# Two heads per stationary matrix in the levels of a blockwise triangular inverse (two hybrid layer stacks, one core)

## What is computed

```python
kk = jnp.einsum("bhnid,bhnjd->bhnij", k_beta, kc)
lower = jnp.eye(c, dtype=f32) + jnp.where(strict, kk * decay, 0.0)
rhs = jnp.concatenate([vc * bc[..., None], k_beta * jnp.exp(G)[..., None]], axis=-1)
uw = lax.linalg.triangular_solve(lower, rhs, left_side=True, lower=True)
```

## Time and profile before

| | |
|---|---|
| median of 3 runs | 2100.92 us (2100.28 to 2102.86) |
| the profiled execution | 2102.94 us, its span 2101.1 us |
| PE busy | 1967.9 us (94% of the span) |
| DVE busy | 802.2 us (38%) |
| ACT busy | 448.8 us (21%) |
| POOL busy | 433.2 us (21%) |
| granted TensorE clock, mean of the span | 0.958 of 2.4 GHz |
| share of the chain that ended last: PE | 87% |
| levels of the first layer of the second stack | 1554.78 to 1616.51 us |
| levels of the second layer | 1950.13 to 2011.86 us |

### The profile page before, as it was taken

The page is one execution under the profiler, slowest core; times in us unless marked ns, Lnnn a source line. Parts: engine busy times, 40 slices in busy tenths (PEclk is TensorE's granted clock), DMA queues, the critical chain, the costliest instruction groups (busy, mean ns, idle before and its releaser), DMA issues.

```text
span 2101.1 us, 25762 instructions
## 1 busy us (share of the span) xinstructions
PE 1967.9 (94%) x10102; PEld 1192.8 (57%) x10102; DVE 802.2 (38%) x1957; ACT 448.8 (21%) x1213; POOL 433.2 (21%) x463
## 2 busy tenths in 40 slices
PE   7999997999996999897989996999999989999997
PEld 4566555555553566555545553546679544556973
DVE  2735345122113734436212123235554323455534
ACT  4333211111112333210111111122310112232011
POOL 0101302433431101311324331001330000024000
PEclk9999897999997999997989998999899999999999
DMA  5121067999933121065999965120020021101100
GB/s 214 35 83 41 0 272 276 422 395 366 375 141 148 54 83 41 1 270 183 415 400 387 393 257 212 40 80 31 31 81 1 32 90 73 48 31 71 41 1 40
DMA packets 52824, 323.39 MB, mean 154 GB/s; under 512 B 20876, under 2 KB 22188, under 8 KB 29920
## 3 DMA queue, kind: packets, MB, share of 16 engines
q1 hardware_dynamic: 33344, 292.28, 35.2%
q0 software_dynamic: 19360, 29.45, 3.9%
HBM read 404.21 MB, written 30.93 MB: 207 GB/s over the span
## 4 chain that ended last, share of the span: by engine, by line
PE 87%; DVE 5%; DMA 4%; ACT 1%; issue 1%; POOL 0%; SPq 0%; POOLq 0%; DVEq 0%; ACTq 0%
PE bank L932 14%; PE bank L562 14%; PE bank L2188 11%; PE bank L2174 8%; PE bank L950 8%; PE bank L574 4%; PE bank L2159 4%; DMA b_nat<-xn_rows,b_rows_ix 3%; PE bank L2349 3%; PE bank L2340 3%; PE bank L548 2%; PE bank L2280 2%; PE bank L914 2%; PE bank L2277 2%; PE bank L2151 1%
## 5 line engine op out<-in xcount | busy, mean ns | idle before, releaser
L932 PE MATMUL bank<-b_arena,b_nat 128*64 128x256 f32 x3008 | 345.8, 383 | 3.7 <-DVE b_nat L1412 3.7
L562 PE MATMUL bank<-b_arena 128*128 128x512 f32 (+2 forms) x768 | 308.6, 556 | 2.6 <-issue 2.2
L932 PEld LDWEIGHTS bank<-b_arena,b_nat 128*64 128x64 f32 x3008 | 219.2, 139 | 154.1 <-issue 61.0
L1412 DVE TENSOR_TENSOR b_nat<-bank,b_prm 128x512 f32<-128x512 f32 x94 | 65.1, 693 | 438.3 <-PE bank L914 330.3
L2188 PE MATMUL bank<-b_actT,b_ring 128*128 128x512 f32 x512 | 224.0, 594 | 0.0
L562 PEld LDWEIGHTS bank<-b_arena 128*128 128x128 f32 x768 | 145.3, 194 | 137.2 <-issue 107.4
L950 PE MATMUL bank<-b_arena,b_ebuf 128*64 128x512 f32 x752 | 185.4, 614 | 1.9 <-ACT b_ebuf L1253 1.9
L2174 PE MATMUL bank<-b_ring,b_actT 128*128 128x384 f32 (+1 forms) x512 | 177.1, 504 | 7.6 <-DVE b_actT L3028 7.6
L2188 PEld LDWEIGHTS bank<-b_actT,b_ring 128*128 128x128 f32 x512 | 96.0, 190 | 114.9 <-issue 113.8
L1385 POOL DMA_INDIRECT y_rows<-b_va,b_rows_ix x94 | 95.8, 1019 | 313.4 <-ACT b_va L1261 305.7
L2174 PEld LDWEIGHTS bank<-b_ring,b_actT 128*128 128x128 f32 x512 | 98.8, 196 | 78.6 <-issue 33.0
(11 more groups left out here) (363 smaller groups left out, 2577.8 us busy)
## 6 DMA issues: line engine op xcount, KB each, us to landing
b_arena<-in_w SPq DMA_DIRECT2D x64, 2048.0 KB, 15.0
b_arena<-in_w SPq DMA_DIRECT2D x64, 1024.0 KB, 17.1
b_ring<-in_w_t SPq DMA_DIRECT2D x8, 2048.0 KB
b_arena<-in_w SPq DMA_DIRECT2D x8, 1536.0 KB, 15.8
b_ring<-in_w_n2b SPq DMA_DIRECT2D x6, 1536.0 KB
b_arena<-in_w_out SPq DMA_DIRECT2D x4, 2048.0 KB
b_arena<-y_rows SPq DMA_DIRECT2D x8, 1024.0 KB, 7.9
b_ring<-in_w_out SPq DMA_DIRECT2D x4, 2048.0 KB
```

The lines of the kernel that those rows point to most:

```text
L562: ins = pe.matmul(bank[:, 0:width], actT[:, k, tok(i)], w[:, k, :], start=k == 0, stop=k == KD - 1)
L932: ins = pe.matmul(psum[2 + b % 2][f * CAP:(f + 1) * CAP, 0:256], xgT[:, b % 2, k % 4, k // 4, :], w[:, k, f, :], start=k == 0, stop=k == K ...
```

## The change

The heads 0 and 1 are paired with the heads 2 and 3. L of one head lies below the diagonal, the transpose of L of the other above it, so the sum of both fits one 128 x 128 matrix. `first_inverse` builds it (`pairs[t]`, two matrices per chunk). For each level GpSimd multiplies it by a mask that now holds the level's blocks on both sides of the diagonal and writes `own[t]` (`level_part`). With it as the stationary matrix, one matmul of 128 columns gives the first product of one head (natural order, its 64 even-block columns) and of the paired head (transposed, its 64 odd-block columns): `mixed` describes these interleaved columns. The mask sits in the stationary matrix, so the product needs no masking, and ScalarE copies it out. A second ScalarE operation (`mix`) gathers the counterpart columns of the inverses into the other half of `t1`, which then serves as stationary and as moving operand. `inv` and `turned` (the transposes) of a chunk now lie side by side in `both[t]`. The copies of bank "lt" on ScalarE go.

The second matmul of the pair works on whole 128-column products: 4 matmuls of 128 columns in place of 8 of 64 (in the last level 4 of 64, as before). The order of PE, of the banks and of the chunks is kept.

```diff
@@ constants
         if n == 0:
             c[:, CN["lvlt"]:CN["lvlt"] + P] = m.T
+        else:
+            c[:, CN["lvl"] + n * P:CN["lvl"] + (n + 1) * P] = m | m.T
@@ block_two
-        lt = [by_heads(y[:, t, 0:DW]) for t in range(T)]
+        pairs = [y[:, t, 0:2 * P].rearrange("p (h s) -> p h s", h=2) for t in range(T)]
...
+        both = [ring[2][:, 2 * t * DW:2 * (t + 1) * DW].rearrange("p (s j) -> p s j", j=P) for t in range(T)]
+        inv = [both[t][:, 0:DH, :] for t in range(T)]
+        turned = [both[t][:, DH:2 * DH, :] for t in range(T)]
+        squares = [ring[2][:, n * DW:(n + 1) * DW] for n in range(4, 8)]
...
+        own = [y[:, t, 2 * P:4 * P].rearrange("p (h s) -> p h s", h=2) for t in range(T)]
...
+        def mixed(heads, n, pair=None):
+            b = 1 << n
+            ap = heads if pair is None else heads[:, pair, :]
+            blocks = (P if pair is None else P // 2) // b
+            return bass.AP(ap.tensor, ap.offset, [list(heads.ap[0]), [2 * b, blocks], [2 * P + b, 2], [1, b]])
@@ level_one (PE)
-                four(l, "t1", lambda h: lt[t][:, h, :], lambda h: inv[t][:, tok(h)], T * (n - 1) + t)
+                s = T * (n - 1) + t
+                pe.wait_ge(*after(l, "own", s + 1))
+                pe.wait_ge(*vacant(l, "t1", s))
+                bank, full = writer(l, "t1", s)
+                for c in range(2):
+                    ins = pe.matmul(bank[:, tok(c)], own[t][:, c, :], mixed(inv[t], n, c), start=True, stop=True)
+                ins.then_inc(*full)
@@ level_two (PE)
                 pe.wait_ge(*emptied(l, "t1", s))
-                if n > 1:
+                if n < LEVELS - 1:
+                    pe.wait_ge(*after(l, "mixed", s + 1))
...
                 if n < LEVELS - 1:
-                    for h in range(DH):
-                        pe.matmul(bank[:, 64 * h:64 * (h + 1)], by_heads(invT[t])[:, h, :],
-                                  level_cols(t1[s % 2][:, h, :], n, 0), start=True, stop=True)
-                for h in range(DH):
-                    ins = pe.matmul(bank[:, 256 + 64 * h:256 + 64 * (h + 1)], t1[s % 2][:, h, :],
-                                    level_cols(invT[t][:, tok(h)], n, 1), start=True, stop=True)
+                    for c in range(2):
+                        pe.matmul(bank[:, tok(c)], t1[s % 2][:, 2 + c, :], t1[s % 2][:, c, :], start=True, stop=True)
+                    for c in range(2):
+                        ins = pe.matmul(bank[:, tok(2 + c)], t1[s % 2][:, c, :], t1[s % 2][:, 2 + c, :],
+                                        start=True, stop=True)
...
@@ run_scalar
-                copy_out(l, "lt", lt[0], 0)
-                copy_out(l, "lt", lt[1], 1)
...
-                for t in range(T):
-                    copy_out(l, "yg", actT[:, DH:KD, tok(t)], t, scale=prm[:, l, PC2["glag"]:PC2["glag"] + 1])
+                def mix(s):
+                    n, t = 1 + s // T, s % T
+                    if n > 1:
+                        act.wait_ge(*after(l, "invT", s - T + 1))
+                    else:
+                        act.wait_ge(*after(l, "inv0", t + 1))
+                    if s >= 2:
+                        act.wait_ge(*filled(l, "up", s - 2))
+                    act.activation(t1[s % 2][:, 2:4, :].rearrange("p c (k w b) -> p (c k) w b", w=2, b=1 << n),
+                                   mixed(turned[t], n), ACT.Copy).then_inc(*did("mixed"))
+                for s in range(T * (LEVELS - 1)):
+                    if s < T * (LEVELS - 2):
+                        mix(s)
+                    copy_out(l, "t1", t1[s % 2][:, 0:2, :], s)
+                    if s % T == T - 1 and s < T * T:
+                        copy_out(l, "yg", actT[:, DH:KD, tok(s // T)], s // T,
+                                 scale=prm[:, l, PC2["glag"]:PC2["glag"] + 1])
@@ run_gpsimd
+            def level_part(l, s):
+                n, t = 1 + s // T, s % T
+                if n > 1:
+                    pool.wait_ge(*filled(l, "t1", s - T))
+                else:
+                    pool.wait_ge(*after(l, "inv0", t + 1))
+                pool.tensor_tensor(own[t], pairs[t], every(lvl[:, n, :], 2), ALU.mult).then_inc(*did("own"))
...
-                for t in range(T):
-                    gate_gla(l, t)
+                for s in range(T * (LEVELS - 1)):
+                    level_part(l, s)
+                    if s % T == T - 1 and s < T * T:
+                        gate_gla(l, s // T)
@@ first_inverse (DVE)
-                link(tt(by_heads(inv[t]), dn[t % 2], every(lvl[:, 0, :]), ALU.mult))
-                link(tt(by_heads(inv[t]), every(ident), by_heads(inv[t]), ALU.subtract))
-                dve.wait_ge(*emptied(l, "lt", t))
-                link(tt(by_heads(invT[t]), lt[t], every(lvl[:, LEVELS, :]), ALU.mult))
-                tt(by_heads(invT[t]), every(ident), by_heads(invT[t]), ALU.subtract).then_inc(*did("inv0"))
+                dve.wait_ge(*filled(l, "lt", t))
+                bank, free = reader(l, "lt", t)
+                lt, d = by_heads(bank[:, :]), dn[t % 2]
+                tt(pairs[t], lt[:, 0:2, :], d[:, 2:4, :], ALU.add)
+                tt(inv[t][:, 2:4, :], lt[:, 2:4, :], every(lvl[:, LEVELS, :], 2), ALU.mult)
+                tt(turned[t][:, 2:4, :], lt[:, 0:2, :], every(lvl[:, LEVELS, :], 2), ALU.mult).then_inc(*free)
+                tt(inv[t][:, 0:2, :], d[:, 0:2, :], every(lvl[:, 0, :], 2), ALU.mult)
+                link(tt(turned[t][:, 0:2, :], d[:, 2:4, :], every(lvl[:, 0, :], 2), ALU.mult))
+                tt(both[t], every(ident, 8), both[t], ALU.subtract).then_inc(*did("inv0"))
@@ levels (DVE)
                 for s in range(T * (LEVELS - 1)):
-                    level_mask(l, s)
-                    if s:
-                        level_update(l, s - 1)
-                level_update(l, T * (LEVELS - 1) - 1)
+                    level_update(l, s)
```

More of the change, by code:

```diff
@@ L2275, in level_two @@
                 if n < LEVELS - 1:
[L2276 to L2281 removed]
+                    for c in range(2):
[4 more added lines that the diff above has]
+                else:
+                    for c in range(2):
+                        pe.matmul(bank[:, tok(c)][:, 64:], turned[t][:, c, :], t1[s % 2][:, c, 64:],
+                                  start=True, stop=True)
+                    for c in range(2):
+                        ins = pe.matmul(bank[:, tok(2 + c)][:, 64:], t1[s % 2][:, c, :], turned[t][:, 2 + c, 64:],
+                                        start=True, stop=True)
                 ins.then_inc(*full)
@@ L2301, in solve @@
                     for h in range(DH):
-                        ins = pe.matmul(bank[:, tok(h)], wT[t][:, h, :], st[:, h, :], start=False, stop=h == DH - 1)
+                        ins = pe.matmul(bank[:, tok(h)], wT(t, h), st[:, h, :], start=False, stop=h == DH - 1)
                 ins.then_inc(*full)
@@ L2978, in level_update @@
                 bank, free = reader(l, "up", s)
-                half = lambda o: bank[:, o:o + 256].rearrange("p (g b) -> p g b", b=1 << n)
                 if n < LEVELS - 1:
-                    cols = level_cols(inv[t], n, 0)
-                    tt(cols, cols, half(0), ALU.subtract).then_inc(*did("inv"))
-                cols = level_cols(invT[t], n, 1)
-                tt(cols, cols, half(256), ALU.subtract).then_inc(*did("invT"))
+                    part = lambda c: bank[:, 2 * c * P:2 * (c + 1) * P].rearrange(
+                        "p (g w b) -> p g w b", w=2, b=1 << n)
+                    cols = mixed(inv[t], n)
+                    tt(cols, cols, part(0), ALU.subtract).then_inc(*did("inv"))
+                    cols = mixed(turned[t], n)
+                    tt(cols, cols, part(1), ALU.subtract).then_inc(*did("invT"))
+                else:
+                    part = lambda c: bank[:, 2 * c * P:2 * (c + 1) * P].rearrange("p (c j) -> p c j", c=2)[:, :, 64:]
+                    cols = inv[t][:, 2:4, 64:]
+                    tt(cols, cols, part(0), ALU.subtract).then_inc(*did("inv"))
+                    cols = turned[t][:, 2:4, 64:]
+                    tt(cols, cols, part(1), ALU.subtract).then_inc(*did("invT"))
                 dve.wait_ge(*after(l, "invT", s + 1))
```

36 lines of the change are left out of this document (15 added, 21 removed).

## The result

| | before | after |
|---|---|---|
| median of the runs timed together | 2101.69 us (2100.28 to 2102.86, 4 runs) | 2049.09 us (2044.52 to 2051.59, 4 runs) |
| the profiled execution, its span | 2102.94, 2101.1 us | 2044.52, 2042.7 us |
| levels of the two layers, from the rows of PE | 61.73, 61.73 us | 33.60, 33.59 us |
| granted clock, mean of the span | 0.958 | 0.958 |

The ratio is 0.9748, with a 95% interval of 0.9729 to 0.9766. The kernel is 2.5% faster: 52.6 us by these medians. The same kernel timed once more (experiment "again") gave 2044.75 us (2042.92 to 2050.52, 5 runs) against 2100.93, a gain of 56.2.

What follows compares the result with a forecast made beforehand. PE was taken to bound the kernel, in the levels through its weight loads. 57.2 - 0.6 - 0.8 = 55.8 us saved from 2102.94 gave 2047.1, or 2045 in terms of the median, range 2041 to 2058.

Steps and rivals of the forecast that it cites:

- The price of a record, and the 57.2 us: PE in the levels: 256 fewer records a layer at 0.1117 us each save 28.6 us a layer, 57.2 in both.
- The short runs of the moving operand: First product at level 1, two-element runs: taken as nothing; at worst 0.45 us a step, 3.6 us in both layers.
- Three semaphores per group: Each level_one group of 4 records passes three semaphores: taken as zero; 0.1 us a step would be 4.8 us.
- DVE and GpSimd side by side: In the levels, DVE's update with one input in PSUM stays at 0.75 us beside GpSimd's new masks.
- GpSimd's and ACT's spare time: Levels, step of 1.34 us: GpSimd needs on average 1.1 us at most, ACT 0.83 with 0.7 us spare.
- rival D: Levels: GpSimd locked out by DVE or slow with the broadcast mask, slower than before; 2135 us at 3 us; chance 0.02.
- The wait ahead of query_sums, 0.6 us: Longer first_inverse makes silu(l, 11) 0.3 us later, so PE waits 0.3 us a layer before query_sums, 0.6 in both.
- The start of the levels, 0.8 us: PE's first level_two waits 0.68 us for ACT, not 0.30: 0.8 in both layers, 0 if ACT's operations overlap.
- The sum: Whole kernel: 55.8 us saved from the profiled 2102.94 us gives 2047.1, or 2045 in terms of the median.
- A: Levels: another engine, likeliest GpSimd at 1.60 us a step, sets the pace and gives back 12.5 us: 2058; chance 0.10.
- B: Levels: PE pays 0.1 to 0.2 us a step per wait or moving run, 2050 to 2055 us; chance 0.12.
- C, the clock: Levels: the granted clock falls and they run at 1.2 GHz, only 6 us saved, 2095 us; chance 0.02.

Runs made afterwards that it cites:

- twice: The changed kernel with every first product and every matmul of levels 1 to 5 issued twice into the same place: 2100.8 us, first layer's levels 61.81 us.
- thin: The changed kernel with an extra one-column matmul ahead of each first product and each matmul of levels 1 to 5: 2104.77 us, first layer's levels 61.70 us.
- pool2: The changed kernel with one more GpSimd multiply of 128x256 in every step of the levels, into an unused buffer: 2041.65 us.
- pool3: As pool2, with one more GpSimd mask of 128x128 a step that nobody reads: 2054.39 us, levels 41.81 and 41.82 us.
- early: The changed kernel with mix(0) and mix(1) ahead of the last tanh of N3, and silu(11) ahead of first_inverse(0): 2046.61 us, ratio 0.9741 to before.
- wide: The changed kernel with the 16 matmuls of query_sums moving 32 columns of ones in place of one: 2037.51 us, ratio 0.9704 to before.

## Why the prediction was right, point by point

- **The price of a record, and the 57.2 us.** Right. 256 records fewer a layer, a step of 1.34 us, PE and weight loads busy but for the start, 512 records fewer in all. The levels measured 33.60 against 33.5 forecast. "twice" and "thin" make it a cause, and not a coincidence: 24 records a step give back 61.7 to 61.8 us, with 1, 64 or 128 columns moving in them.
- **The short runs of the moving operand.** Zero was nearly right. In level 1, where the trace of before left up to 0.45 us a step open, the distance from one `level_one` to the next is 1.38 us (1555.14 to 1556.52), in the next 1.34 (to 1557.86). That is 0.04 us a step, some 0.3 us in both layers. The Trainium skill's lines of 16 bytes with two accesses each (SBUF — State Buffer, Specifications), read strictly as a charge for every new line, would have cost up to 3.6 us at this level; the trace, with a tenth of that, speaks against that reading.
- **Three semaphores per group.** Zero was right: 1.34 us a step is 12 records at the price of before.
- **DVE and GpSimd side by side.** The update stayed at 0.75 us with GpSimd at 0.72 to 0.73 beside it. The Trainium skill (SBUF — State Buffer, SBUF: two separate sides) has DVE and GpSimd share one pair of ports, which a DVE operation needs if both its inputs are in SBUF. By that rule the update, with one input in PSUM, runs free, and the trace agrees. "pool2" agrees as well: GpSimd at 93% of the stage left DVE's 16.58 us as they were.
- **GpSimd's and ACT's spare time.** Enough, as forecast, with more room than the sum gave: a gate took 1.27 us and not 1.60. The point from which GpSimd decides was put at 2.57 us a mask in rival D; that is where the kernel would be slower than before. The point where it begins to cost anything is far lower ("pool3").
- **The wait ahead of query_sums, 0.6 us.** Wrong: 0. `silu` and `square` do come later, by what was worked out: a chunk of `first_inverse` takes 2.93 us (2.95 forecast). But the step from a later weight load to a later matmul failed. The loads wait 0.39 us and PE's matmuls follow the projection group after the same 10.33 us. The loads of before had been 0.33 us ahead of their matmuls (1508.69 and 1509.02), and that lead took up the 0.26 us. I had read the start of the weight loads as that of the matmuls.
- **The start of the levels, 0.8 us.** Right in kind, a third in size: a wait of 0.44 us in place of 0.30, where 0.68 was forecast, so 0.3 us in both layers. ACT's operations overlap at their ends (1551.18 + 0.49 is 1551.67, and `mix` starts at 1551.57), as the prediction had as its lower case. The start of `level_two` comes 1.36 us after that of the levels, where 1.58 was forecast. "early" takes 0.24 away.
- **The sum.** 56.3 us by stages, against 55.8 with the two waits. The forecast of 2045.0 us lies inside the runs (2044.52 to 2051.59); the median of the first four is 4.1 us above it, that of the next five 0.3 below. So the stage was forecast to 0.1 us, and the whole no better than its scatter allows: that a median of the changed kernel came within 0.3 us is luck. The prediction treated everything outside the levels as fixed. It is not: the clock moves one stretch by 1.6 us from profile to profile, and the first stack by up to 10 us for a reason that the profiles don't show.
- **The rivals.** A, B and D did not come about. C, the clock, did not touch the levels (1.00 in every window of them shown here), but it was right to look at the earlier trace rows: the clock falls behind the thin matmuls one stage earlier, and "wide" shows that they are the reason.

## What to carry to other kernels

Where PE and its weight-load column are both full and no matmul moves more than 128 columns, count stationary matrices and not columns: two half-used products merged into one stationary matrix nearly halved the stage, while the same work with the old number of weight loads gained nothing. With 384 columns a record took 0.323 us, and there such a merger would save only as many columns as it removes (an inference, not run). When the work goes to other engines, ask for each not only whether its share of a step fits but how far ahead its inputs allow it to run; that lead let GpSimd double its work unnoticed. And look at the granted clock behind a run of matmuls that move one column: widening them to 32 cost no time here and took 1.6 to 3.3 us off the stretch behind.

## What the runs showed of the hardware that was not expected

- A float32 matmul with a 128 x 128 stationary matrix costs 0.223 us (two records of 0.1117) with 1, 64 or 128 moving columns, also when the same matrix is loaded twice running ("twice", "thin"). A record of 384 columns takes 0.323 us.
- 16 matmuls of one column in a row are followed by a fall of the granted clock from 2.4 towards 1.2 GHz (0.50 in a window of 4 us before, 0.67 after), although PE's row is busy all the while. With 32 columns it stays at 1.00. With one-column matmuls that alternate with full ones it stays at 1.00, too.
- GpSimd multiplies 128x256 in 0.72 us beside a busy DVE, and starts the next 0.69 us later. The gate of 128x512 took 1.27 to 1.28 us in the changed kernel. Its 1.60 us in the earlier trace rows is a mean of two prices in the kernel before: in each layer three gates of 1.71 to 1.73 us beside DVE operations with both inputs in SBUF, and a fourth of 1.26 to 1.27 us behind them.
